# Middle stage of a hybrid encoder: transfers over two queues, a new order on TensorE, a mask by matmul, a fused bias and maximum

## The reference

```python
proj = hp @ w_in[l]                       # first stage
# gated delta rule, 8 heads of 64, state S per head
A = jnp.where(strict, beta[..., :, None] * kk * decay, 0.0)   # decay = exp(G_i - G_j), causal
T = A + jnp.eye(chunk)                    # W, U: triangular solves with T
u = U_c - W_c @ S
o = qd_c @ S + qk_c @ u                   # qk already times decay
S = gt_c * S + kd_c.T @ u
o = o * rsqrt(mean(square(o)) + eps) * norm_w * silu(z)
# sliding window attention, 8 query heads, 2 key heads, learned sinks
s = q @ k.T * 64 ** -0.5 + bias           # bias shared, -inf outside the window
p = softmax(concatenate([s, sink]))[..., :-1];  o2 = p @ v
# third part: output projection, layer norm, MLP
h = layer_norm(ALPHA * h + concatenate([o, o2]) @ w_o)
h = layer_norm(ALPHA * h + square(relu(h @ w_ff1)) @ w_ff2)
```

## Time and profile before

| | |
|---|---|
| median of 3 runs | 3069.74 us (3067.99 to 3071.34) |
| the profiled execution | 3076.34 us, span 3074.6 us |
| TensorE busy | 2767.8 us, 90% of the span |
| VectorE, ScalarE, GpSimd busy | 42%, 30%, 45% |
| mean granted TensorE clock | 0.94 |
| middle stage | 620 to 1570 us of the span |

### The profile page before, as it was taken

One profiled execution on the slowest core, in us unless ns is written; L12 is line 12 of the kernel. 1 busy time (PEld: TensorE's weight loads), 2 busy tenths in 40 slices (PEclk: granted clock), 3 DMA queues, 4 the chain that ended last, 5 costly groups with the idle time before them and its releaser, 6 DMA issues. The chain is left out here.

```text
span 3074.6 us, 50904 instructions
## 1 busy us (share of the span) xinstructions
PE 2767.8 (90%) x17616; PEld 2613.6 (85%) x17616; DVE 1297.9 (42%) x2325; ACT 928.6 (30%) x1982; POOL 1389.6 (45%) x1876
## 2 busy tenths in 40 slices
PE   5899999925988998899669999999999999999996
PEld 5899999914776776777559999999999999999996
DVE  7643300124765666666245314621561166126402
ACT  4322211312443444444222222222222222222222
POOL 4201110014445555655135555555555556555554
PEclk9899999956998998999779999999999999999998
DMA  5322221152332333233133434444344444434432
GB/s 199 107 87 89 74 81 67 53 125 71 87 107 77 90 99 106 81 86 93 54 125 116 139 126 127 132 137 130 121 144 130 127 135 134 127 124 135 133 116 85
DMA packets 225873, 336.63 MB, mean 109 GB/s; under 512 B 78362, under 2 KB 161498, under 8 KB 222954
## 3 DMA queue, kind: packets, MB, share of 16 engines
q1 hardware_dynamic: 224730, 333.81, 35.1%
q10 hardware_dynamic: 1056, 1.70, 0.2%
HBM read 265.67 MB, written 69.78 MB: 109 GB/s over the span
## 5 line engine op out<-in xcount | busy, mean ns | idle before, releaser
L1963 POOL TENSOR_TENSOR c_w_lo<-c_raw,c_w_hi 128x512 fp32r<-128x512 f32 x640 | 852.3, 1332 | 640.2 <-ACT c_w_hi L1983 639.5
L1983 ACT ACTIVATE c_w_hi<-c_raw 128x512 fp32r<-128x512 f32 x640 | 404.4, 632 | 1057.2 <-PE c_bank L124 1024.5
L122 PE MATMUL c_bank<-c_h_hi,c_w_hi 128*128 128x416 f32 x1280 | 454.1, 355 | 21.7 <-POOL c_w_lo L1963 20.5
L124 PE MATMUL c_bank<-c_h_hi,c_w_lo 128*128 128x416 f32 x1280 | 452.8, 354 | 0.0
L124 PE MATMUL c_bank<-c_mid_hi,c_w_lo 128*128 128x416 f32 x1280 | 450.8, 352 | 0.0
L122 PE MATMUL c_bank<-c_mid_hi,c_w_hi 128*128 128x416 f32 x1280 | 450.2, 352 | 0.0
L123 PE MATMUL c_bank<-c_h_lo,c_w_hi 128*128 128x416 f32 x1280 | 449.1, 351 | 0.0
L123 PE MATMUL c_bank<-c_mid_lo,c_w_hi 128*128 128x416 f32 x1280 | 447.0, 349 | 0.0
L122 PE MATMUL a_bank<-a_h_hi,a_w_hi 128*128 128x420 f32 (+4 forms) x984 | 341.9, 347 | 6.0 <-PEq L168 4.5
L124 PE MATMUL a_bank<-a_h_hi,a_w_lo 128*128 128x420 f32 (+4 forms) x984 | 340.5, 346 | 0.0
L123 PE MATMUL a_bank<-a_h_lo,a_w_hi 128*128 128x420 f32 (+4 forms) x984 | 340.2, 346 | 0.0
(11 more groups left out here) (226 smaller groups left out, 4193.8 us busy)
## 6 DMA issues: line engine op xcount, KB each, us to landing
c_raw<-in_w_ff SPq DMA_DIRECT2D x320, 512.0 KB, 3.5
scratch_proj<-a_row SPq DMA_DIRECT2D x22, 1152.0 KB, 5.1
b_qkv<-scratch_proj SPq DMA_DIRECT2D x18, 768.0 KB, 7.0
a_raw<-in_w_in SPq DMA_DIRECT2D x23, 512.0 KB, 5.8
a_x<-in_x SPq DMA_DIRECT2D x18, 512.0 KB, 3.6
scratch_h_rows<-a_h SPq DMA_DIRECT2D x18, 512.0 KB, 2.7
b_lane_a<-scratch_at_lanes SPq DMA_DIRECT2D x72, 128.0 KB, 2.7
b_res<-scratch_h_rows SPq DMA_DIRECT2D x18, 512.0 KB, 3.9
```

Source lines behind the costliest of these rows:

```text
L122: pe.matmul(out, w_hi, x_hi, start=first, stop=False)
L124: return pe.matmul(out, w_lo, x_hi, start=False, stop=last)
L1963: pool.tensor_tensor(w_lo[:, p % 2, ks, :], raw[:, p, ks, :], w_hi[:, p % 2, ks, :].bitcast(F32), ALU.subtract).then_inc(w_lo_done, 1)
L1983: act.activation(w_hi[:, p % 2, ks, :], raw[:, p, ks, :], ACT.Copy).then_inc(w_hi_done, 1)
```

## The change

- Transfers: the store of `at` for the lanes moves from the SP queue to the ScalarE queue (`to_lanes`), the load stays on SP (`load_lanes`). SP's step now begins with `from_lanes(t)`, then `load_lanes(n)`, and the rest behind; `from_lanes(START)` leaves the loads of `w_o`; the exchange of the state comes before `from_lanes` in the last step.
- TensorE: a new order. `turn_o` moves into the next tile's step; `from_state` goes behind `key_products`; `query_products` and the attention rows of the output product's second half come earlier; `turn_probs` moves ahead of `pair_rows`, `scores` ahead of `solve_rest`, `attend` ahead of `state_update`. The gates use the bank `prod`, the pair rows the bank `one2`.
- Mask: `exponents` is gone. TensorE adds the causal mask by a product of an identity with the mask (`mask_future`), accumulating with `spread_gates`; ScalarE takes exponentials from PSUM; `e_left` is the last column of `decay`.
- Bias and maximum: `tensor_tensor_reduce` per head gives the biased scores and their maximum with the sink; the bias is scaled by 8 once. `maxima` is left with two small operations and moves one tile ahead.
- `low` moves from GpSimd to VectorE.

The diff, cut to its core:

```diff
-            def to_lanes(t):
-                sp.wait_ge(s["at_done"], by(t, 2))
-                for b in range(BLOCKS32):
-                    here = slice(b * SMALL, b * SMALL + SMALL)
-                    sp.dma_start(io["at_lanes"][b * HEADS:b * HEADS + HEADS, :, :].rearrange("h j i -> j h i"),
-                                 at[here, t.parity, :, here]).then_inc(s["at_out"], 16)
+            def load_lanes(t):
...
+                if not t.loop and t.n < 2:
+                    load_hidden(t.n + 1)
                 if t.last():
                     change_state()
+                from_lanes(t)
+                if n:
+                    load_lanes(n)
                 load_z(t)
-                if t.reaches(1):
-                    load_res(t.plus(-1))
                 if m2:
                     load_front(m2)
                 if t.reaches(2):
                     store_rows(t.plus(-2))
-                if n:
-                    to_lanes(n)
-                if t.reaches(2):
                     store_cols(t.plus(-2))
-                if not t.loop and t.n < 2:
-                    load_hidden(t.n + 1)
+                load_res(t)
                 if not t.loop and t.n == TILES - 3:
                     store_window(n, "k_prompt", "v_prompt")
                 if not t.loop and t.n == TILES - 2:
                     store_window(n, "k_sample", "v_sample")
                 if m2:
                     load_attention(m2)
-                if n:
-                    from_lanes(n)
 
...
-            to_lanes(START)
+            load_lanes(START)
             load_front(START.plus(1))
             load_hidden(0)
             for k in range(2, KT):
-                if k == 6:
-                    from_lanes(START)
                 sp.wait_ge(s["wo_lo_done"], k - 1)
                 sp.dma_start((x1, h1)[k % 2][:, :], io["w_o"][k]).then_inc(s[f"wo_in{k % 2}"], 16)
...
+            def mask_future(t):
+
+                if t.reaches(1):
+                    pe.wait_ge(s["s_biased"], by(t.plus(-1), 2))
+                else:
+                    pe.wait_ge(s["mask_copied"], 2)
+                pass_waits(pe, s["passed"])
+                for g in range(2):
+                    pe.matmul(heads4(fr[g]), ident_r[:, :], per_head(future_r[:, :], 4), start=True, stop=False)
+
...
-                        last = pe.matmul(fr[g][:, j * P:j * P + P], pick[rows, j, :], cum_row[rows, :], start=True, stop=True)
+                        last = pe.matmul(fr[g][:, j * P:j * P + P], pick[rows, j, :], cum_row[rows, :], start=False, stop=j == 3)
                 last.then_inc(s["gb_full"], 1)
 
             def key_products(t):
-                pe.wait_ge(s["em_done"], by(t, 6))
+                pe.wait_ge(s["decay_done"], by(t, 2))
...
-                if j == 1:
-                    pe.wait_ge(s["x_done"], by(t, 2))
-                    if n:
-                        pe.wait_ge(s["kd_done"], by(n, 2))
+                if n and j == 1:
+                    pe.wait_ge(s["v_done"], by(n, 2))
+                    pe.wait_ge(s["kd_done"], by(n, 2))
                 elif n:
+                    pe.wait_ge(s["kd_done"], by(n, 2))
                     pe.wait_ge(s["qk_scaled"], by(n, 1))
...
-                from_state(t)
+                    mask_future(n)
+                    spread_gates(n)
+                if chain:
+                    turn_o(p)
                 if n:
-                    spread_gates(n)
                     turn_queries(n)
                 if chain:
-                    output_product(p, 0, ATTENTION)
+                    output_product(p, 0, ATTENTION, n)
                 if n:
                     key_products(n)
+                from_state(t)
+                if chain:
+                    output_product(p, 0, DELTA)
+                if n:
+                    query_products(n)
+                if chain:
+                    output_product(p, 1, ATTENTION)
                 if norm:
                     turn_h1(pp, 0, n)
-                if chain:
-                    output_product(p, 0, DELTA)
+                turn_probs(t, 0)
                 pair_rows(t)
+                turn_probs(t, 1)
+                pair_update(t)
                 if norm:
                     turn_h1(pp, 1)
                 if chain:
-                    output_product(p, 1, ATTENTION)
-                pair_update(t)
-                if n:
-                    query_products(n)
+                    output_product(p, 1, range(0, 2))
                 solve_head(t)
                 if chain:
-                    output_product(p, 1, range(0, 2))
+                    output_product(p, 1, range(2, 4))
                 carry_over(t)
-                if chain:
-                    output_product(p, 1, range(2, 4))
+                if n:
+                    scores(n)
                 solve_rest(t)
-                turn_probs(t, 0)
-                turn_probs(t, 1)
+                attend(t)
                 state_update(t)
                 output_update(t)
-                if n:
-                    scores(n)
-                attend(t)
+                turn_attention(t)
                 if n:
                     turn_values(n)
-                turn_o(t)
-                turn_attention(t)
 
...
-            def exponents(t):
-                dve.wait_ge(s["gb_full"], by(t, 1))
-                for g in range(2):
-                    hs = slice(4 * g, 4 * g + 4)
-                    dve.tensor_tensor(decay[:, hs, :], heads4(fr[g]), per_head(future, 4), ALU.add).then_inc(s["em_done"], 1)
-                    at_end = heads4(fr[g])[:, :, P - 1]
-                    dve.tensor_tensor(ends[:, 0, hs], at_end, cum[:, 0, hs], ALU.subtract).then_inc(s["em_done"], 1)
-                    dve.tensor_copy(ends[:, 1, hs], at_end).then_inc(s["em_done"], 1)
 
...
-                    dve.tensor_tensor(kd[:, t.parity, hs, :], turned_heads(1, g), across(e_left[:, hs], HD), ALU.mult).then_inc(s["kd_done"], 1)
+                    dve.tensor_tensor(kd[:, t.parity, hs, :], turned_heads(1, g), across(decay[:, hs, P - 1], HD), ALU.mult).then_inc(s["kd_done"], 1)
...
             def biased(t):
                 dve.wait_ge(s["scored"], by(t, 1))
+                pass_waits(dve, s["passed"])
                 for half in range(2):
-                    for c in range(2):
-                        hs = slice(4 * half + 2 * c, 4 * half + 2 * c + 2)
-                        last = dve.scalar_tensor_tensor(probs[:, hs, :], heads4((fr, inv)[half][c], SPAN), HD ** -0.5,
-                                                        bias[:, hs, :], ALU.mult, ALU.add)
+                    for c in range(4):
+                        h = 4 * half + c
+                        source = (fr, inv)[half][c // 2][:, c % 2 * SPAN:c % 2 * SPAN + SPAN]
+                        last = dve.tensor_tensor_reduce(probs[:, h, :], source, bias[:, h, :], HD ** -0.5, sinks[:, h:h + 1],
+                                                        ALU.add, ALU.max, soft[:, 1, h:h + 1])
                     last.then_inc(s["s_biased"], 1)
...
-                    hide(HIDING.index(t.n))
-                dve.tensor_reduce(soft[:, 0, :], probs[:, :, :], AX.X, ALU.max).then_inc(s["soft_steps"], 1)
-                dve.wait_ge(s["soft_steps"], by(t, 4, 1))
-                dve.tensor_tensor(soft[:, 1, :], soft[:, 0, :], sinks[:, :], ALU.max).then_inc(s["soft_steps"], 1)
-                dve.wait_ge(s["soft_steps"], by(t, 4, 2))
+                    number = HIDING.index(t.n)
+                    hide(number)
+                    dve.tensor_reduce(soft[:, 0, :], probs[:, :, :], AX.X, ALU.max).then_inc(s["soft_hidden"], 1)
+                    dve.wait_ge(s["soft_hidden"], 2 * number + 1)
+                    dve.tensor_tensor(soft[:, 1, :], soft[:, 0, :], sinks[:, :], ALU.max).then_inc(s["soft_hidden"], 1)
+                    dve.wait_ge(s["soft_hidden"], 2 * number + 2)
...
                     copy_gates(n)
-                if n:
                     copy_sums(n)
+                if chain:
+                    sum_squares(p)
+                    low(p, ATTENTION, 1)
+                    normalise_o(p)
                 if n:
                     sum_keys(n)
-                residue(t)
+                if chain:
+                    gate_o(p)
+                if t.reaches(2):
+                    norm_gain(t.plus(-2))
                 if n:
                     strengths(n)
-                    exponents(n)
                     scale_values(n)
-                    sum_queries(n)
+                if chain:
+                    low(p, DELTA, 2)
+                if n:
                     decayed_keys(n)
-                turn_even(t)
+                residue(t)
                 if chain:
                     residual(p, 0)
-                copy_pair_rows(t)
                 if n:
                     left_keys(n)
-                maxima(t)
+                    decayed_queries(n)
+                    sum_queries(n)
```

(70 more changed lines are left out.)

94 lines of the change are left out of this document (55 added, 39 removed).

## The result

The changed kernel takes 2985.18 us (median of four, 2983.35 to 2990.43), the kernel before 3070.54 us in the same session: ratio 0.9724, 95% interval 0.9707 to 0.9741. That is faster by 85 us. The forecast was 2996 us, 74 us faster. The profiled execution of the changed kernel took 2990.43 us around its span of 2988.6 us, so the two spans differ by 86.0 us.

The account below looks back on a forecast made before the run. A ring through GpSimd's queue, 44.1 of the 44.23 us tile, was taken as the bound. Gains of 44 (tiles) + 15 (start-up) + 11 (last tile) + 4 (end) = 74 us gave 3069.74 - 74 = 2996 us; 8 in 10: 2958 to 3036.

Parts of the forecast that it names:

- The ring: Middle-stage tiles: output product waits for GpSimd's `mix_lo`, queued behind the inverses; moving `low` to VectorE removes it, 44 us gained.
- rival 3: Middle-stage tiles: ring closes again through lanes and inverses, 5.6 us slack; 3034 us if contention ate 8; 0.19 with Rival 2.
- The sum of the ring: One old middle-stage tile: 8.3 + 25.35 + 1.25 + 5.41 + 3.8 = 44.1 of its 44.23 us.
- The tile: Steady middle-stage tile: 39.8 us at full clock, 41.0 with a 2.5 us clock fall in half the tiles.
- The new wait: TensorE at `turn_o(p)`, waiting for `normalise_o(p)`: 1.5 us once a tile, replacing the old wait.
- The fused operation: VectorE's bias and maximum per head: 0.40 us each, 3.2 us a tile, bounds 0.34 to 0.68 per head.
- It is just covered: VectorE needs 7.1 us from `scored` to the end of `scale_attention`; TensorE meanwhile has 7.8 us of work.
- Contention: Both `low` on VectorE beside GpSimd's inverses: one blocked 0.6 us at each would stretch the inverses, not TensorE.
- Rival 2: VectorE becomes the bound in the tiles: fused operation 0.68 per head or `low` slowed; 3032 us; 0.19 with rival 3.
- Rival 4: ScalarE queue: four slow issues block the exponentials; at 3 us each 3122 us, slower than before; chance 0.07.
- Start-up: Before the first step: VectorE's 17.64 us wait for w_o mostly goes, masking hidden under loads; 15 us gained, bounds 10 to 17.6.
- Last tile and end: Last tile: 12.60 us state wait goes, masking moves a step earlier, 11 us gained (8 to 15); end: 4 (2 to 6).

Follow-up runs that it names:

- experiment 6: Changed kernel with the fused bias-and-maximum undone (four 512-column operations, then one maximum over 2048 columns): 3025.74 us, ratio 0.9847.
- experiment 8: Changed kernel with `turn_o(p)` moved behind `turn_queries(n)` and the attention half of the first output product: 3023.15 us, ratio 0.9838.
- experiment 4: Changed kernel with `low` put back on GpSimd, ahead of the next tile's inverses: 3108.3 us, ratio 1.0116.
- experiment 5: Changed kernel with the four stores of `at` issued by SP again, none on the ScalarE queue: 2987.3 us, ratio 0.9718.
- experiment 9: Kernel of experiment 8 with `norm_gain(t-2)` moved ahead of `gate_o(p)` on VectorE: 2966.81 us, ratio 0.9656.
- experiment 10: Changed kernel with `maxima(START)` and its masking moved behind the fourth split of w_o: 2983.72 us, ratio 0.9708.
- experiment 11: Kernel of experiment 9 with hidden-key masking of three tiles moved to TensorE as one-row products behind each score product: 3012.36 us, ratio 0.9800.

## Why the prediction was right, and where its reasons were not

- **The ring.** The prediction said that "the tile is paced by a ring in which GpSimd's queue joins two unrelated things", and gave all 44 us of the tiles to moving `low`. That step failed as an explanation: with `low` alone moved the tile was 44.47 us, since a second ring through SP's queue, nearly as long, took over. Moving `low` and reordering the queues together gives 46 us in the tiles. The number came out by luck in part, because the change also reorders SP, whose new ring I had walked under rival 3. I had walked it for slack in the new order and not for its length in the old.
- **The sum of the ring.** That five terms added up to 44.1 of 44.23 us proves less than it seemed. The 25.35 us of the inverses were not measured: I had added TensorE's tile of 44.23 us to the start of `low`, so the sum had to come out near 44.23. GpSimd's own rows have the next `low` here:
```profile
1119.17 2.70 POOL L1745 TENSOR_TENSOR b_mix_lo<-b_mixed,b_mix_hi 128x512 fp32r<-128x512 f32 x2
```
The inverses took 23.5 us, the ring is 42.3, and from `low` to `low` it is 42.4. So it does close in this tile, but the tile is not the usual one. Over the tiles the inverses take 23.2 to 24.9 us, mostly 23.5, while the way from `at` to their start takes 7.3 to 13.1 us, 10.6 on average for the 8.3 taken; the two errors nearly cancel.
- **The tile.** Forecast 39.8 us without a fall of the clock and 41.0 on average; measured 38.7 without, 40.2 with one, and 40.0 on average. The new wait is 1.1 to 1.2 us for 1.5 (its terms add up to 4.8 and not 4.9, so 1.4 by the prediction's own rows). TensorE is busy for 36.8 us of a tile at full clock, the mask included, for the 37.6 taken; the mask costs nothing, since it fills a wait, and the rest of that gain was not split. Nine of fifteen tiles fall, where half were taken, but a fall costs 1.5 us and not 2.5. The average of 40.0 holds the sixteenth step, which takes 45.0 us. Hence 60.3 us for 44, the largest miss, inside the bounds of 24 and 64.
- **The fused operation.** Taken as 0.40 us per head, measured 0.405. The Trainium skill ("VectorE: DVE Perf Modes", section "Two Vector instructions with no wait between them") says that such an operation is two instructions; the trace agrees, with a read-out of 0.084 us that the next head's operation overlaps. "It is just covered" was right, and experiment 6 shows how little cover there was. The forecast did not price this edit as a gain; undone, it costs 40 us.
- **Contention.** The Trainium skill ("SBUF — State Buffer", section "Who interferes with whom") says that a Vector operation with two SBUF inputs contends with a GpSimd operation that reads SBUF, and the trace agrees. I had priced it at 0.6 us on the inverses. It struck elsewhere: 1.9 us on VectorE's own subtraction beside `h1_rows`, hidden behind the key products in the changed kernel (the row at 1042.75) and on the path in experiment 8. Rival 2 was wrong for the changed kernel and is the cause one edit away from it.
- **Lanes.** Rival 3's slack of 5.6 us is about 8: loads issued by 1043.36, landing taken as 2 us, wanted at 1053.67.
- **ScalarE queue.** The four issues take 1.81 us in the steady tile for the 2.0 taken, with no wait behind them. Rival 4's slow issues did occur, once, at the start (13.67 us for four behind the store of the skewed bias), where ScalarE had nothing else to do.
- **Start-up.** 15 forecast, 10.3 measured. The wait of 17.64 us shrank to 2.14, which is what was forecast for it. "Falls while it waits for loads" held for half of the masking only: block 2 was ready for VectorE at 691.14 and the masking ended at 693.53, 2.4 us later. Another 1.1 us is lost at the last two blocks, and the first split already lay 1.65 us later, at a place that moves by more than that between kernels that share the code up to there (676.5 to 680.0). Step 0 gave back 3.9 us that I had not counted. The clock explains it: it stayed at 0.50 for the whole step and TensorE was busy 7.9 us longer than before. With the same work on TensorE in this step, in the traces of three kernels (after, experiments 4 and 8) the clock is 0.50 throughout and the step takes 47.3 us; in those of experiments 5, 6, 9 and 10 it rises on the way, to a mean of 0.62 to 0.66, and the step takes 42.3 to 43.7. What decides between the two stays open.
- **Last tile and end.** 11 forecast for the last tile, 16.6 measured. No wait for the state is left. The 4.6 us that the forecast gave back for the masking are right, but fall in the step before, where TensorE waits 4.5 us at `turn_attention`; they are counted there. Without that term the forecast for the last tile is 12.6 + 3 = 15.6. The end gave 2.1 for 4, the lower bound.
- **The queues.** That a second queue helps, the headline of the change, is shown to be wrong for the changed kernel.

## What to carry to other kernels

When a chain of waits names one releaser, work out the length of every other ring through the same buffers before crediting its removal: two rings that differ by a few per cent hide each other, and only an edit of both shows. Take every term of such a sum from the engine's own rows; a term got from the length of the tile makes the sum come out by itself. Before moving a short operation to another engine, look at what long operation of a third engine it will then stand beside. A product laid where its engine must wait anyway is free, and one that breaks a side-by-side pattern costs far more than its columns.

## What the runs showed of the hardware

- A VectorE subtraction of 128x512 with two inputs in SBUF took 2.50 to 2.55 us beside a GpSimd addition of 128x1024 (changed kernel, experiment 8), and 0.67 us when the two were apart (experiment 9).
- The granted clock fell from 0.98 to 0.50 amid one-row products with no idle time ahead of it (experiment 11). With a wait of 1.1 to 1.2 us a tile it fell in nine of fifteen tiles, with waits of 0.6 us in none of fifteen.
- The same step of the same work took 42.3 us at a mean granted clock of 0.66 and 47.3 us at 0.50.
- Eight score products on two halves of the partitions took 1.9 us side by side; with one-row products between them each of the sixteen took 0.62 us at full clock and 1.15 at half.
